# Two RMS norms between products from partial square sums, one root and scaling transposes, and q/k norm weights folded away

## The reference, cut to what matters

```python
# end of block 1, start of block 2 (block 2 takes the normed x as its residual)
x  = _rmsnorm(x + silu(g) * u @ w_down, final_norm_w)
h  = _rms(x, g_norm1) * (1 + sc1) + sh1
proj = h @ w_in                                   # c_q, c_kv, k_pe, q_sb, k_sb, v_sb, gates
q  = _rms((_rms(c_q, g_q_latent) @ w_uq).reshape(B, S, 8, 192), g_q_head)
kv = (_rms(c_kv, g_kv_latent) @ w_ukv).reshape(B, S, 8, 256)
k  = _rms(concat(kv[..., :128], k_pe), g_k_head)  # then rope on the last 64 of q and k
...                                               # two attentions, gates, w_out
x  = x + gt1 * (merged @ w_out)
h2 = _rms(x, g_norm2) * (1 + sc2) + sh2           # into the feed-forward gu2, dn2
```

## Time and profile before

| | before |
|---|---|
| median of three runs | 2746.18 us |
| the profiled execution | 2746.09 us |
| its span, first to last instruction | 2744.2 us |
| mean granted PE clock | 0.991 |
| PE busy | 2677.9 us, 98% of the span |
| DVE, ACT busy | 1754.4 us (64%), 1298.9 us (47%) |
| loads and stores | 581.56 MB, mean 212 GB/s |

### The profile page before, as it was taken

How to read it: one execution, slowest core, us unless ns; L and a number is a source line. 1 busy time by engine, 2 the same in 40 slices (tenths; PEclk the granted TensorE clock), 3 DMA queues, 4 the chain that set the end, 5 groups by cost and what they waited for, 6 DMA issues and landing times.

```text
span 2744.2 us, 33836 instructions
## 1 busy us (share of the span) xinstructions
PE 2677.9 (98%) x12421; PEld 2213.1 (81%) x12421; DVE 1754.4 (64%) x2047; ACT 1298.9 (47%) x1512; POOL 3.2 (0%) x9
## 2 busy tenths in 40 slices
PE   8999999999999999999799999999899999999999
PEld 6888888878888888877577788888678888887877
DVE  5788668476776767787675554575577644445565
ACT  5555544354344444443555555644344443444443
POOL 0000000000000000000000000000000000000000
PEclk9999999999999999999899999999999999999999
DMA  7766555688788888887565455555478766555555
GB/s 250 248 202 191 147 156 164 197 273 282 272 283 272 284 272 281 275 274 232 153 198 157 150 160 170 169 183 179 145 262 284 242 192 189 185 183 184 184 184 168
DMA packets 302099, 581.56 MB, mean 212 GB/s; under 512 B 19933, under 2 KB 20309, under 8 KB 301733
## 3 DMA queue, kind: packets, MB, share of 16 engines
q1 hardware_dynamic: 300912, 576.34, 65.3%
q10 hardware_dynamic: 740, 2.27, 0.2%
q0 software_dynamic: 336, 1.46, 0.2%
HBM read 577.89 MB, written 2.10 MB: 211 GB/s over the span
## 4 chain that ended last, share of the span: by engine, by line
PE 93%; DVE 4%; ACT 2%; issue 1%; DMA 0%; SPq 0%; ACTq 0%; DVEq 0%
PE acc L341 29%; PE acc L343 28%; PE acc L342 28%; DVE lo L330 1%; PE ex L979 1%; PE aux L1000 1%; PE tp L1356 1%; PE aux L539 1%; DVE op_lo L468 0%; ACT xn L409 0%; PE tp L448 0%; ACT hi L324 0%; PE aux L1961 0%; ACT stage L460 0%; PE aux L1960 0%
## 5 line engine op out<-in xcount | busy, mean ns | idle before, releaser
L330 DVE TENSOR_TENSOR lo<-raw,hi 128x1024 fp32r<-128x1024 f32 x895 | 1077.7, 1223 | 511.3 <-ACT hi L324 491.4
L324 ACT ACTIVATE hi<-raw 128x1024 fp32r<-128x1024 f32 x895 | 927.7, 1055 | 679.0 <-PE acc L343 548.7
L341 PE MATMUL acc<-hi,op_hi 128*128 128x512 f32 x2752 | 1089.3, 396 | 21.5 <-DVE lo L330 19.7
L343 PE MATMUL acc<-hi,op_lo 128*128 128x512 f32 x2752 | 1075.0, 391 | 0.0
L342 PE MATMUL acc<-lo,op_hi 128*128 128x512 f32 x2752 | 1074.2, 390 | 0.0
L341 PEld LDWEIGHTS acc<-hi,op_hi 128*128 128x128 f32 x2752 | 518.4, 188 | 135.0 <-issue 24.5
L343 PEld LDWEIGHTS acc<-hi,op_lo 128*128 128x128 f32 x2752 | 518.1, 188 | 109.8
L342 PEld LDWEIGHTS acc<-lo,op_hi 128*128 128x128 f32 x2752 | 518.8, 189 | 103.0 <-issue 0.2
L341 PE MATMUL acc<-hi,f_hi 128*128 128x512 f32 x704 | 279.0, 396 | 2.5 <-DVE xres L1461 1.3
L343 PE MATMUL acc<-hi,f_lo 128*128 128x512 f32 x704 | 277.8, 395 | 0.0
L342 PE MATMUL acc<-lo,f_hi 128*128 128x512 f32 x704 | 277.7, 395 | 0.0
(11 more groups left out here) (293 smaller groups left out, 1410.6 us busy)
## 6 DMA issues: line engine op xcount, KB each, us to landing
raw<-w_in SPq DMA_DIRECT2D x257, 512.0 KB, 3.9
ada_ring<-w_ada SPq DMA_DIRECT2D x192, 512.0 KB, 5.1
raw<-w_gate_up SPq DMA_DIRECT2D x176, 512.0 KB, 4.9
raw<-w_ffn_in SPq DMA_DIRECT2D x176, 512.0 KB, 4.6
raw<-w_down SPq DMA_DIRECT2D x88, 512.0 KB, 5.6
raw<-w_ffn_out SPq DMA_DIRECT2D x88, 512.0 KB, 4.3
raw<-w_out SPq DMA_DIRECT2D x64, 512.0 KB, 4.3
raw<-w_proj_mla SPq DMA_DIRECT2D x16, 512.0 KB, 4.2
```

The source lines that it names most:

```text
L324: A.activation(hi[:, k, :, 0:n], raw[:, k, :, 0:n], ACT.Copy).then_inc(hi_ready, 1)
L330: V.tensor_tensor(lo[:, k, :, 0:n], raw[:, k, :, 0:n], hi[:, k, :, 0:n].bitcast(F32), ALU.subtract).then_inc(lo_ready, 1)
L341: T.matmul(dst, lh, hi[:, k, kk, 0:n], start=first and kk == 0, stop=False)
L343: mm = T.matmul(dst, ll, hi[:, k, kk, 0:n], start=False, stop=last and kk == CK - 1)
```

## The change

The work on the norms is taken apart and redistributed.

- **Squares in pieces.** ACT squares x and the weighted rows piece by piece (`part_squares`) as blocks of x become final, into `parts`. The first half is done in step 38 of dn1 (DVE multiplies that half by the weights in step 37), the third quarter after the third block's readout, the last quarter after the fourth. For out2, three quarters are squared after the readouts of its first three blocks.
- **One root for two norms.** With r = rsqrt(mean(x^2) + eps) and xw = x * w, the second norm of r * xw is xw * rsqrt(mean(xw^2) + eps * (mean(x^2) + eps)). DVE computes both variances, ACT takes both roots in one instruction. The root's table is loaded earlier by a dummy root (`root_table`).
- **Scaling inside the transpose.** DVE multiplies the identity by the row scale (`turned`), and PE makes the first four groups as products of the unscaled rows with this diagonal, in fp32. Groups 4 to 7 are scaled into `xn` and transposed as before. The residual x is scaled at chunks G = 9 and 10.
- **Split ahead.** ACT and DVE split the first three chunks of in2 and of gu2 before the norm, DVE two of them before the last blocks' readouts and the third behind them.
- **Middle readouts.** In dn1 and dn2 the readout of block m stands right behind the split of chunk (22, m).
- **Queries and keys.** The weights of the first 128 columns go into a per-column scale of an ACT copy (L1648, now two instructions); those of the rotated 64 columns go into the tables of sines and cosines. The full multiplication of the queries is gone. Sums, rotation and the keys' squares are spread over more chunks.
- Two small weight rows are loaded at the start. The vector of the second norm's modulation is formed earlier.

The core of the diff:

```diff
+        HALF = D // 2
+        def part_squares(act, src, kind, t, j, c, junk, n):
+            A.activation(junk[:, 0:c.stop - c.start], src[:, t, c], ACT.Square, accum_out=parts[:, kind, t, j:j + 1]).then_inc(part_done, 1)
+            act.wait_ge(part_done, n)
+        def root_table(act):
+            A.activation(small[:, 4, 31:32], cols[:, 0:1], ACT.Sqrt)
+        def act_norm_root(act, n, w):
+            act.wait_ge(var_ready, n)
+            A.activation(small[:, 3, 0:w], small[:, 2, 0:w], ACT.Sqrt).then_inc(root_ready, 1)
+        def dve_norm_root(dve, cd, n, w):
+            v, r, y, tmp = (small[:, j, 0:w] for j in (1, 2, 3, 4))
+            V.reciprocal(r, v).then_inc(var_ready, 1)
+            dve.wait_ge(root_ready, n)
+            cd.done(V.tensor_tensor(tmp, y, y, ALU.mult))
+            cd.done(V.tensor_tensor(tmp, tmp, v, ALU.mult))
+            cd.done(V.tensor_scalar(tmp, tmp, -0.5, 1.5, ALU.mult, ALU.add))
+            cd.done(V.tensor_tensor(y, y, tmp, ALU.mult))
+        def dve_norm_spread(dve, src):
+            for t in range(TT):
+                ins = V.tensor_scalar(turned[:, t], ident, small[:, 3, t:t + 1], None, ALU.mult)
+            ins.then_inc(norm_diag, 1)
+            for t in range(TT):
+                V.tensor_scalar(xn[:, t, HALF:], src[:, t, HALF:], small[:, 3, t:t + 1], None, ALU.mult).then_inc(norm_scaled, 1)
...
+        def pe_normed(pe, op, src, n):
+            def operand(g):
+                G = OG[op] + g
+                pe.wait_ge(stage_ready, CK * (G - 1))
+                if g < 4:
+                    pe.wait_ge(norm_diag, n)
+                else:
+                    pe.wait_ge(norm_scaled, TT * n)
+                for kk in range(CK):
+                    for t in range(TT):
+                        c = (CK * g + kk) * P
+                        dst = tp[:, G % 2, kk * S + t * P:kk * S + (t + 1) * P]
+                        if g < 4:
+                            ins = T.matmul(dst, src[:, t, c:c + P], turned[:, t], start=True, stop=True)
+                        else:
+                            ins = T.transpose(dst, xn[:, t, c:c + P], ident)
+                ins.then_inc(tp_ready, 1)
+            operand(0)
+            operand(1)
...
+                if 0 < k < 7:
+                    operand(k + 1)
+                if k < 8:
+                    pe.wait_ge(op_ready, OG[op] + k + 1)
...
+        AHEAD = 3
+        def act_ahead(act, name, ks):
+            for k in ks:
+                act_chunk(act, CH[name] + k, 0, 16)
+        def dve_ahead(dve, name, ks):
+            for k in ks:
+                dve_chunk(dve, CH[name] + k, 0, 16)
...
+                if n == 1 and j == 38:
+                    root_table(act)
+                    act.wait_ge(x_added, 2)
+                    for t in range(TT):
+                        part_squares(act, x, 0, t, 0, slice(0, HALF), xn[:, 0], 1 + t)
+                    act.wait_ge(xw_ready, TT)
+                    for t in range(TT):
+                        part_squares(act, xw2, 1, t, 0, slice(0, HALF), xn[:, 0], 3 + t)
...
-                    if (j, m) in ((22, 1), (23, 0)):
-                        readout(0, 1 - m)
+                    if j == 22:
+                        readout(0, m)
...
+                    dve.wait_ge(s_row, 16)
+                    dve.wait_ge(x_added, 2)
+                    dve.wait_ge(chunk_used, c0 + 2 * 34)
+                    for t in range(TT):
+                        V.tensor_tensor(xw2[:, t, 0:HALF], x[:, t, 0:HALF], wrow[:, 0:HALF], ALU.mult).then_inc(xw_ready, 1)
+            dve_ahead(dve, "in2" if n == 1 else "end", range(2 if n == 1 else 0))
...
+                for t in range(TT):
+                    V.tensor_tensor(x[:, t, c], x[:, t, c], acc[:, p, t], ALU.add).then_inc(x_added, 1)
+                    dve.wait_ge(x_added, 4 + t)
+                    V.tensor_tensor(xw2[:, t, c], x[:, t, c], wrow[:, c], ALU.mult).then_inc(xw_ready, 1)
+                dve.sem_inc(acc_free[p])
             return f
...
+        def act_norm_first(act):
+            c2, c3 = slice(2 * NB, 3 * NB), slice(3 * NB, D)
+            junk = xn[:, 0]
+            act.wait_ge(x_added, 3)
+            for t in range(TT):
+                part_squares(act, x, 0, t, 1, c2, junk, 5 + t)
+            act.wait_ge(xw_ready, TT + 1)
+            for t in range(TT):
+                part_squares(act, xw2, 1, t, 1, c2, junk, 7 + t)
+            for t in range(TT):
+                act.wait_ge(x_added, 4 + t)
+                part_squares(act, x, 0, t, 2, c3, junk, 9 + 2 * t)
+                act.wait_ge(xw_ready, TT + 2 + t)
+                part_squares(act, xw2, 1, t, 2, c3, junk, 10 + 2 * t)
+            act_norm_root(act, 3, 4)
+        def dve_norm_first(dve, cd):
+            dve.wait_ge(part_done, 12)
+            ss, v, tmp = small[:, 0, 0:4], small[:, 1], small[:, 4, 0:TT]
+            cd.done(V.tensor_reduce(ss, parts[:, :, :, 0:3].rearrange("p k t j -> p (k t) j"), AX_X, ALU.add))
+            cd.done(V.tensor_scalar(v[:, TT:4], ss[:, 0:TT], 1.0 / D, EPS, ALU.mult, ALU.add))
+            cd.done(V.tensor_scalar(tmp, ss[:, TT:4], 1.0 / D, None, ALU.mult))
+            cd.done(V.scalar_tensor_tensor(out=v[:, 0:TT], in0=v[:, TT:4], scalar=EPS, in1=tmp, op0=ALU.mult, op1=ALU.add))
+            dve_norm_root(dve, cd, 3, 4)
+            dve_norm_spread(dve, xw2)
...
-                A.activation(m_qk[:], tp[:], ACT.Copy).then_inc(ml["qk"], 1)
+                A.activation(m_qk[:, :, 0:S], tp[:, :, 0:S], ACT.Copy, scale=cols[:, C_GQH:C_GQH + 1]).then_inc(ml["qk"], 1)
+                A.activation(m_qk[:, :, S:], tp[:, :, S:], ACT.Copy).then_inc(ml["qk"], 1)
...
-                act_chunk(act, C2 + G, 0, 4)
+                if G >= AHEAD:
+                    act_chunk(act, C2 + G, 0, 4)
...
+                    A.activation(k_sq[:, :, 0:6], kvv[:, :, 0:6, 0:NOPE], ACT.Square).then_inc(ml["sq"], 1)
                 if G == G_SB + 2:
-                    act.wait_ge(ml["q"], 1)
...
-                    A.activation(k_sq, kvv[:, :, :, 0:NOPE], ACT.Square).then_inc(ml["sq"], 1)
+                    A.activation(k_sq[:, :, 6:8], kvv[:, :, 6:8, 0:NOPE], ACT.Square).then_inc(ml["sq"], 1)
...
+                if G == G_OUT + 26:
+                    root_table(act)
+                for b in range(3):
+                    if G == G_OUT + 8 * b + 11:
+                        act.wait_ge(added, b + 1)
+                        for t in range(TT):
+                            part_squares(act, x, 0, t, b, slice(b * NB, (b + 1) * NB), xn[:, 1], 13 + 2 * b + t)
...
+                if G >= AHEAD:
+                    dve_chunk(dve, C2 + G, 0, 4)
+                if G in (9, 10):
+                    t = G - 9
+                    V.tensor_scalar(x[:, t], xw2[:, t], small[:, 3, TT + t:TT + t + 1], None, ALU.mult).then_inc(x1_ready, 1)
...
+                if G == G_UP + 7:
+                    lo_gain, hi_gain = (m_gq[:, h * 32:h * 32 + 32].unsqueeze(1).to_broadcast([P, TT, ROPE // 2]) for h in range(2))
+                    for dst, src, gain in ((2, 1, lo_gain), (3, 0, hi_gain), (0, 0, lo_gain), (1, 1, hi_gain)):
+                        cd.done(V.tensor_tensor(m_ang[:, dst], m_ang[:, src], gain, ALU.mult))
+                if G in (G_UP + 9, G_UP + 10):
+                    t = G - G_UP - 9
                     dve.wait_ge(ml["sq"], 1)
-                    for t in range(TT):
-                        ins = V.tensor_reduce(small[:, 0, 8 * t:8 * t + 8], q_sq[:, t].rearrange("p (h n) -> p h n", h=HEADS), AX_X, ALU.add)
-                    ins.then_inc(ml["sum"], 1)
-                if G == G_UP + 10:
-                    cd.done(V.tensor_tensor(qv, qv, m_gq[:].unsqueeze(1).unsqueeze(1).to_broadcast([P, TT, HEADS, QH]), ALU.mult))
-                if G == G_UP + 11:
-                    dve.wait_ge(ml["sum"], 1)
-                    dve_rope(cd, qv[:, :, :, NOPE:QH], HEADS).then_inc(ml["q"], 1)
-                if G == G_SB + 2:
+                    V.tensor_reduce(small[:, 0, 8 * t:8 * t + 8], q_sq[:, t].rearrange("p (h n) -> p h n", h=HEADS), AX_X, ALU.add).then_inc(ml["sum"], 1)
+                if G in (G_UP + 11, G_UP + 12):
+                    dve.wait_ge(ml["sum"], TT)
+                    dve_rope_products(cd, qv[:, :, :, NOPE:QH], HEADS, (2, 3, 0, 1), (0, 1) if G == G_UP + 11 else (2, 3))
+                if G == G_UP + 13:
+                    dve_rope_sums(cd, qv[:, :, :, NOPE:QH], HEADS).then_inc(ml["q"], 1)
...
+            dve_ahead(dve, "gu2", range(2))
```

190 lines of the change are left out of this document (102 added, 88 removed).

## The result

| kernel | median, us | runs | ratio to before, 95% interval |
|---|---|---|---|
| before | 2745.78 | 4, 2744.72 to 2748.47 | |
| after | 2723.88 | 4, 2721.34 to 2724.53 | 0.9917 (0.9900 to 0.9934) |
| after, measured again | 2722.31 | 5, 2721.40 to 2723.80 | 0.9915 (0.9902 to 0.9929) |

The forecast was 2720.0 with a range of 2713 to 2728. The change gave 22 to 23.5 us where my sum had 26.1. The profiled execution took 2724.53 (span 2722.5).

What follows compares the result with a forecast made beforehand. PE, busy 98% of the span, was taken as the bound, so only its work and waits count. The terms -10.9 - 4.2 - 1.0 - 7.8 - 2.6 + 0.4 = -26.1 took 2746.1 to 2720.0 us, range 2713 to 2728.

Steps and rivals of the forecast that it cites:

- Norm 1: After dn1, T being PE's end there: first product of in2 at T + 11.65 instead of T + 22.6, -10.9 us.
- Norm 2: After out2, T2 being PE's end there: first product at T2 + 10.75 instead of T2 + 15.0, -4.2 us.
- Behind both norms: Chunks after each norm: half the low-clock cost goes, less added diagonal records; -0.5 each, -1.0 us, bounds -3 to +2.
- Queries and keys: Waits of 3.6 and 3.0 us and 1.7 of low clock go, 0.5 remains: -7.8 us, bounds -3 to -8.3.
- Rival 1: ACT becomes the late one in queries and keys, which give 3 instead of 7.8: 2725 us; chance 0.14.
- Middle readouts: Middle of dn1 and dn2: readout moved first removes two waits of 1.3 us, -2.6 us.
- Put in: Steps 37 and 38 of dn1: added DVE work, table load and squares make the next `lo` late, +0.4 us (0 to 1.5).
- What I had at 0: Start and remaining stretches: no change forecast; two more row loads at the start lie in idle time, 0.
- 2 (four records): Diagonal products at the norms cost four records, not two, some +7 us: 2727 us; chance 0.05.
- 3 (the low clock stays): Low clock does not end behind the norms, at most +50 on -26: up to 2770 us; chance 0.04.
- 4: Norm chain not shortened, only readouts and keys give: 2736 us, chance 0.04; or nothing gives: 2746, chance 0.02.
- the signs of being wrong: First wait over 10 us, `lo` waits in up and in2b above 3 us, or low clock outlasting the second fed chunk.

Runs made afterwards that it cites:

- r0: The kernel after, nothing edited, measured once more: 2722.31 us.
- e4: The kernel after with the spacer `align` 8 floats shorter, so `big` and all behind it lie 32 bytes lower in SBUF: 2706.19 us (0.9856).
- e6: The kernel before with its spacer `align` 32 floats (128 bytes) longer, no instruction changed: 2732.90 us (0.9952).
- e2b: The kernel after with products nobody reads filling PE's waits, 30 ahead of norm 1 and 26 ahead of norm 2: 2717.88 us (0.9898).
- e1: The kernel after without diagonal products: VectorE scales `xn` in pieces and all groups are transposed: 2722.17 us (0.9914).
- e3: The kernel after with queries and keys put back as before the change, without the two added row loads: 2716.22 us (0.9893).
- e7: From e4: unread products in the norms' waits (28, 27), transposes for diagonals, last part squared by DVE, dn1's wide squares spread over four steps: 2701.54 us (0.9836).
- e12: e7 plus six more unread products between each norm's first two operands and the first product: 2699.28 us (0.9830).

## Why the prediction was right, and where it was off

- **Norm 1, -10.9.** Measured -10.9, step for step: the reciprocal at T + 5.3 for T + 5.5, the operand at 7.27 for 7.35, the product at 11.66 for 11.65. A record of the diagonals took 3.75 / 16 = 0.23 us at the low clock, for 0.22.
- **Norm 2, -4.2.** -4.4. VectorE's third split is the late one, as I had it: it starts at 1958.69, takes 1.22, and the sum follows it at once.
- **Behind both norms, -1.0.** This term was mis-sized: +1.2 in the profiled pair, -0.7 with r0 in the place of after, +0.5 for e4 and e6. I took it that with a shorter wait the products would meet half of the low clock. Before, 3.7 us at norm 1 lay between the first product and the clock's rise; after, from 1313.90 to 1318.41, 4.5 us, and 3.9 in r0, though the wait was 9 us shorter. At norm 2 it was 5.6 before, 3.8 after and none in r0, so how much of the low clock the products meet differs from profile to profile, and the half was a guess. The price of the clock at both norms is what e2b gave back, 3.7 us against r0 and 5.7 against after; that of the diagonals' second records, less the scaling that e1 puts in VectorE's way, is some 1.6 us at norm 1 (e1), near the 0.9 I had here and the 0.9 in the first operand. The term lay within the bounds, -3 and +2.
- **Queries and keys, -7.8.** -8.4, and -9.1 at equal places, beyond my best bound of 8.3: with the better places the 14 chunks of up take 38.2 us for 39.2 in the kernel after, but only 44.4 for 44.7 in the one before, where DVE's queue sets the pace. Rival 1 (ACT late) is out: 0.3 us of wait is left. e3, against e4, puts the part at 10.0 us in the medians, the second fall of the clock in it.
- **Middle readouts, -2.6.** -2.8, and -3.2 at equal places.
- **Put in, +0.4.** +0.8 to +1.1, within 0 to 1.5; e7 took all of it away.
- **What I had at 0.** The step that failed is that a buffer more costs nothing. `parts`, the wider `align` and two columns in `cols` moved the down projections' stationary operand by 160 bytes, from one slow place to a slower one: (2.800 - 2.789) times 88 chunks is 1.0 us in each projection. With the rest, 0.5 us between the queries and the end of out2, where other stationary operands had moved too, this is the drift (some of it falls in the rows of the readouts and the squares): the rows behind the start for which I had 0 sum to 2.2 us in the table, and to 0.2 at equal places. I had read no row for it, though the trace of the kernel before has them: products by `f_hi` take 393 ns there (above, from 2630 us on), and products by `op_hi` of the same shape, from 700 to 900 us, 389:

```profile
L342 PE MATMUL acc<-lo,op_hi x284: 387/389/395, 699.7 to 899.5; 128*128 128x512 f32 x142
```

- **What was luck.** In the profiled pair little: the terms that gave more than forecast make 1.0 us, those that gave less 5.3. That e4 less e6, -26.8, comes so near to -26.1 is luck in part: a start earlier by 1.1, which is no part of the program, and 1.9 more from the queries and the readouts stand against 1.5 less behind the norms and 0.7 less for the squares.
- **Rivals.** 2 (four records) is out with x16 for eight products. 3 (the low clock stays) is out: the clock rose within the first fed chunk, 4.5 and 3.8 us after its start. 4 is out: PE's first operand comes at T + 7.27. None of the signs of being wrong showed.

Of TensorE and transposes the prediction named a section of the Trainium skill, TensorE: Matmul & The Clock Gate, Part 4: PE-mode transpose, that transposes do not count as PE work for the clock. The profiles of e7 and e12 are in line with it: with 28 products in the wait and then eight transposes and 1.8 us of idle time the clock fell; with six products in that idle time it did not; with diagonals for transposes (e2b) it didn't fall even without them. These edits changed the idle time too (1.5 us in e2b), so that the transposes alone do it is not shown. Nor did the diagonals bring the clock back sooner, clear of what two profiles of one program differ by: it was low for 13.7 and 10.2 us in after, 10.2 and 6.8 in r0, and 10.2 and 10.2 in e1, with transposes.
